# Output jobs of one unit moved behind the next unit's query jobs, x loaded transposed, two job banks

## The reference, cut to what matters

```
h    = rms_norm(x, norm_gain)
proj = h @ w_in                       # 5632 columns: aq ak av ag | rq rk rv rg
attn = window_attention(aq, ak, av)   # 16 heads of 64, 4 key/value heads, chunks of 64, window of 2 chunks,
                                      # q and k normed per head, bias -slope*|distance|, one sink per head
ret  = retention(rq, rk, rv)          # 8 heads, q/k 64 wide, v 128 wide, state carried from chunk to chunk,
                                      # group norm per head
out  = x + concat(attn * silu(ag), ret * silu(rg)) @ w_out
```

## Time and profile before

| | |
|---|---|
| Time, median of 3 runs | 1658.97 us (1658.12 to 1659.2) |
| The profiled execution, its own time | 1657.89 us |
| Its span, from the first to the last instruction | 1656.1 us |
| Mean granted clock of TensorE, share of full speed | 0.996 |
| PE busy | 1598.1 us (96%) |
| DVE busy | 1166.8 us (70%) |
| ACT busy | 673.7 us (41%) |
| POOL busy | 450.8 us (27%) |

### The profile page before, as it was taken

How to read it: one execution, slowest core, us unless ns; L and a number is a source line. 1 busy time by engine, 2 the same in 40 slices (tenths; PEclk the granted TensorE clock), 3 DMA queues, 4 the chain that set the end, 5 groups by cost and what they waited for, 6 DMA issues and landing times.

```text
span 1656.1 us, 24605 instructions
## 1 busy us (share of the span) xinstructions
PE 1598.1 (96%) x8320; PEld 1380.1 (83%) x8320; DVE 1166.8 (70%) x3045; ACT 673.7 (41%) x1985; POOL 450.8 (27%) x453
## 2 busy tenths in 40 slices
PE   5999999999999999999999999999999999999999
PEld 5778788787798888888888898888888888888887
DVE  6887768867868576684776757576686766757576
ACT  6543635535444242432444334241444414334241
POOL 5546446454412111121211212121121111212111
PEclk9999999999999999999999999999999999999999
DMA  9748567575774443546357353443547445353451
GB/s 309 280 147 309 200 215 267 185 249 206 245 293 145 176 180 125 200 156 216 125 196 286 135 203 139 170 191 118 213 171 267 181 173 189 129 203 133 171 197 51
DMA packets 151453, 320.49 MB, mean 194 GB/s; under 512 B 26272, under 2 KB 89888, under 8 KB 151328
## 3 DMA queue, kind: packets, MB, share of 16 engines
q1 hardware_dynamic: 151328, 318.91, 53.9%
HBM read 247.56 MB, written 71.30 MB: 193 GB/s over the span
## 4 chain that ended last, share of the span: by engine, by line
PE 51%; DVE 29%; ACT 13%; issue 5%; POOL 1%; DMA 0%; SPq 0%; DVEq 0%; ACTq 0%
PE jb L902 15%; PE jb L904 15%; PE jb L903 14%; ACT sx L417 6%; DVE sx L632 3%; DVE m L635 3%; DVE sx L630 2%; DVE qS L610 2%; DVE d L640 2%; DVE pTL L560 1%; DVE rawqn L603 1%; DVE rawqn L600 1%; ACT qS L400 1%; POOL rstd L303 1%; PE s L975 1%
## 5 line engine op out<-in xcount | busy, mean ns | idle before, releaser
L902 PE MATMUL jb<-wH,hTH 128*128 128x512 f32 (+1 forms) x1024 | 373.8, 365 | 0.0
L903 PE MATMUL jb<-wL,hTH 128*128 128x512 f32 (+1 forms) x1024 | 372.0, 363 | 0.0
L904 PE MATMUL jb<-wH,hTL 128*128 128x512 f32 (+1 forms) x1024 | 371.9, 363 | 0.0
L902 PE MATMUL jb<-wH,mxH 128*128 128x512 f32 x512 | 206.7, 404 | 10.8 <-DVE mxL L560 10.7
L904 PEld LDWEIGHTS jb<-wH,hTL 128*128 128x128 f32 x1024 | 192.8, 188 | 20.5
L902 PEld LDWEIGHTS jb<-wH,hTH 128*128 128x128 f32 x1024 | 193.4, 189 | 18.6
L903 PEld LDWEIGHTS jb<-wL,hTH 128*128 128x128 f32 x1024 | 193.0, 188 | 18.2
L902 PE MATMUL jb<-hTH,wH 128*128 128x512 f32 x512 | 203.4, 397 | 4.0 <-DVE gate L653 4.0
L903 PE MATMUL jb<-hTL,wH 128*128 128x512 f32 x512 | 201.2, 393 | 0.0
L904 PE MATMUL jb<-hTH,wL 128*128 128x512 f32 x512 | 201.1, 393 | 0.0
L904 PE MATMUL jb<-wH,mxL 128*128 128x512 f32 x512 | 200.6, 392 | 0.0
(11 more groups left out here) (148 smaller groups left out, 2973.6 us busy)
## 6 DMA issues: line engine op xcount, KB each, us to landing
wH<-scrH SPq DMA_DIRECT2D x144, 512.0 KB, 7.4
wL<-scrL SPq DMA_DIRECT2D x144, 512.0 KB, 8.1
scrH<-wH SPq DMA_DIRECT2D x48, 512.0 KB, 5.3
scrL<-wL SPq DMA_DIRECT2D x48, 512.0 KB, 6.0
wH<-scrH SPq DMA_DIRECT2D x48, 384.0 KB, 5.8
wL<-scrL SPq DMA_DIRECT2D x48, 384.0 KB, 6.5
stage<-w_in_dram SPq DMA_DIRECT2D x64, 256.0 KB, 4.5
acc<-x_dram SPq DMA_DIRECT2D x4, 2048.0 KB, 15.2
```

The costliest lines, as they stand in the source:

```text
L902: pe.matmul(o, lh, rh_, start=i == 0, stop=False)
L903: pe.matmul(o, lh, rl_, start=False, stop=False)
L904: m = pe.matmul(o, ll, rh_, start=False, stop=i == last)
```

## The change

- The order of the jobs. Unit 0 does query, gate, value jobs. Units 1 to 14 do their query jobs, then the 8 output jobs of the unit before, then their gate and value jobs. Unit 15 does query, gate and value jobs, then the output jobs of 14 and of 15. The jobs still alternate between two banks.
- The steps. The end of the retention of the unit before (A 3, I 2, I 3, MT 0 and 1) stands between the query jobs of this one, MT 2 and 3 and the score steps of this unit between the output jobs. DVE, ACT and POOL have new orders to fit, one part for the query jobs (`qkv_phase`), one for the output jobs, one for gate and value jobs (`late_phases`).
- x. A host-made transposed copy `xT` is loaded to `xt`. PE transposes only the broadcast scale of a tile (`XB`, 1 transpose for each tile instead of 8), DVE multiplies `xt` by gain and scale (`h`), ACT makes the H part in two instructions for a tile, POOL (in block 0 DVE) the L part in two.
- Weights are laid out by panel in HBM by the host, so that a chunk of a panel is one transfer instead of up to three; `stage` has 3 chunks instead of 4. The two weight buffers go by the order of the panels.
- `bias` is 256 columns wide; the mask of the first chunk of block 0 is a DVE memset in units 0 to 3. The small softmax tiles (`m4`, `nm4`, `d4`, `den`, `es`, `rc`) have a copy for even and odd t; `qS` has 2 instead of 4. The scores' two halves stay in separate columns of PSUM, as before.
- `tr` is freed by whichever of TQ and MT used it last (`tr_free`).

```diff
+def phases(n):
+    if n == 0:
+        return [("Q", 0), ("G", 0), ("V", 0)]
+    if n < LAST:
+        return [("Q", n), ("O", n - 1), ("G", n), ("V", n)]
+    return [("Q", n), ("G", n), ("V", n), ("O", n - 1), ("O", n)]
...
+STEPS_MID = {("Q", 0): [("A", -1, 3)], ("Q", 1): [("I", -1, 2), ("MT", -1, 0)], ("Q", 2): [("MT", -1, 1), ("I", -1, 3)],
+             ("Q", 3): [("TQ", 0, 0)],
+             ("O", 0): [("TQ", 0, 1)], ("O", 1): [("MT", -1, 2), ("S", 0, 0)], ("O", 2): [("MT", -1, 3)],
+             ("O", 3): [("TQ", 0, 2), ("S", 0, 1)], ("O", 5): [("TQ", 0, 3), ("PT", 0, 0)],
+             ("O", 6): [("S", 0, 2)], ("O", 7): [("PV", 0, 0)],
+             ("G", 0): [("PT", 0, 1), ("S", 0, 3)], ("G", 3): [("PV", 0, 1), ("PT", 0, 2)],
+             ("V", 0): [("PV", 0, 2)], ("V", 1): [("PT", 0, 3), ("A", 0, 0)],
+             ("V", 2): [("PV", 0, 3), ("A", 0, 1), ("I", 0, 0)], ("V", 3): [("A", 0, 2), ("I", 0, 1)]}
...
 POOL
+            def qkv_phase(n):                       # m = n - 1
+                wl(m, 3, (0, 1)); ggm(m, 3)
+                rpow(n, 0); gpow(m, 1); wl(m, 3, (2, 3))
+                rpow(n, 1); gpow(m, 2); wl(m, 3, (4, 5))
+                rpow(n, 2); wl(m, 3, (6, 7)); gpow(m, 3)
+                rpow(n, 3)
...
 ACT
+            def ocopy(n, t):                        # as before: waits for s_mr of t - 1
+            def qkv_phase(n):
+                rvg(m, 3); ocopy(m, 1); rh(m, 2); wh(m, 3, (0, 1))
+                qkv(n, 0); rh(m, 3); kwh_ah(m, 3); mth(m, 0); ocopy(m, 2); wh(m, 3, (2, 3))
+                qkv(n, 1); mth(m, 1); ocopy(m, 3); wh(m, 3, (4, 5))
+                qkv(n, 2); tqh(n, 0); wh(m, 3, (6, 7))
+                qkv(n, 3); tqh(n, 1); mth(m, 2)
...
+                exps(n, 0); wh(n, 1, (0, 1)); mth(n - 1, 3)
+                tqh(n, 2); exps(n, 1); wh(n, 1, (2, 3))
+                tqh(n, 3); pth(n, 0); exps(n, 2); wh(n, 1, (4, 5))
+                pth(n, 1); wh(n, 1, (6, 7))
...
 DVE
+            def h(b, t):
...
+                for k in range(KT):
+                    i = v.scalar_tensor_tensor(out=xt[:, t % 2, k], in0=xt[:, t % 2, k], scalar=ngain[:, k:k + 1],
+                                               in1=factor, op0=ALU.mult, op1=ALU.mult)
...
+            def qkv_phase(n):
+                rvg(m, 3); kw_am(m, 3); gna(m, 1); rl(m, 2)
+                if n % NU == 0:
+                    h(n // NU, 3)
+                qkv(n, 0); rupd(m, 2); rl(m, 3); kwl_al(m, 3); gnv(m, 1); mtl(m, 0); gnb(m, 1); gna(m, 2)
+                qkv(n, 1); gnv(m, 2); mtl(m, 1); rupd(m, 3); carry_in(n); gnb(m, 2); gna(m, 3)
+                qkv(n, 2); gnv(m, 3); tql(n, 0)
+                qkv(n, 3); tql(n, 1); mtl(m, 2); gnb(m, 3)
+            def late_phases(n):
+                add(n - 1, 7); ptl(n, 1); part1(n, 3); part2(n, 2); carry_out(n); agg(n, 0); rl(n, 0)
+                part2(n, 3); agg(n, 1)
+                mix(n, 0)
+                rq_decay(n)
+                mix(n, 1); ptl(n, 2)
+                mix(n, 2)
+                rvg(n, 0); ptl(n, 3); kw_am(n, 0); kwl_al(n, 0)
+                rvg(n, 1); mix(n, 3); rupd(n, 0); kw_am(n, 1); rl(n, 1); kwl_al(n, 1); gna(n, 0)
+                rvg(n, 2); gnv(n, 0); rupd(n, 1); kw_am(n, 2); kwl_al(n, 2); gnb(n, 0)
...
+            for n in range(1, LAST):
+                qkv_phase(n)
+                part1(n, 0); add(m, 0); mtl(m, 3); add(m, 1)
+                tql(n, 2); part1(n, 1); add(m, 2); part2(n, 0); add(m, 3)
+                tql(n, 3); add(m, 4); ptl(n, 0); part1(n, 2); add(m, 5); part2(n, 1); add(m, 6)
+                late_phases(n)
...
 PE
             def bank_free(n, j):
+                i = JOB_AT[n, j]                    # waits for the reader of the job two before in the new order
...
+            def tr_free():
+                if tr_user[0]:
+                    pe.wait_ge(S[tr_user[0][0]], tr_user[0][1])
...
-            def XT(b, t):
-                for k in range(KT):
-                    m = pe.transpose(xbanks[t % 2][k // 4][:, (k % 4) * P:(k % 4 + 1) * P],
-                                     xbuf[t % 2][:, k * P:(k + 1) * P], ident[:, :])
+            def XB(b, t):
+                pe.transpose(bank, xr[:, t:t + 1].broadcast_to([P, P]), ident[:, :]).then_inc(S["s_xb"], 1)
```

More of the change, by code:

```diff
@@ L252, in units @@
[L252 to L269 removed]
+                    sp.wait_ge(S["s_acc"], b * 32 + 24 + 2 * (t + 1))
@@ new lines, in _ @@
+            xpow(0, 0)
+            wl(0, 0, range(4))
+            xpow(0, 1)
+            wl(0, 0, range(4, 8))
+            xpow(0, 2)
+            xpow(0, 3)
+            qkv_phase(0)
+            late_phases(0)
+            for n in range(1, LAST):
+                qkv_phase(n)
+                if n % NU == 2 and n // NU < NB - 1:
+                    for t in range(NT):
+                        xpow(n // NU + 1, t)
+                wl(n, 1, range(8))
+                late_phases(n)
+            n, m = LAST, LAST - 1
@@ new lines, in _ @@
+            v.wait_ge(S["s_gains"], 16)
+            xms_(0, 0)
+            h(0, 0)
+            xms_(0, 1)
+            xl_first(0)
+            h(0, 1)
+            xl_first(1)
+            xms_(0, 2)
+            xms_(0, 3)
+            h(0, 2)
+            xl_first(2)
+            v.wait_ge(S["s_qkg"], 64)
+            carry_in(0)
+            qkv(0, 0)
+            h(0, 3)
+            xl_first(3)
+            qkv(0, 1)
+            qkv(0, 2); tql(0, 0)
+            qkv(0, 3); tql(0, 1); part1(0, 0)
@@ new lines, in _ @@
+            agg(0, 0); tql(0, 2); part2(0, 0); part1(0, 1)
+            agg(0, 1); tql(0, 3); part2(0, 1); rq_decay(0); ptl(0, 0); part1(0, 2)
+            mix(0, 0); ptl(0, 1); part2(0, 2); part1(0, 3); carry_out(0)
+            mix(0, 1); rl(0, 0); ptl(0, 2); kw_am(0, 0); kwl_al(0, 0); rvg(0, 0); part2(0, 3)
+            mix(0, 2); ptl(0, 3); kw_am(0, 1); rvg(0, 1); rupd(0, 0); rl(0, 1); kwl_al(0, 1); gna(0, 0)
+            mix(0, 3); rvg(0, 2); gnv(0, 0); rupd(0, 1); kw_am(0, 2); kwl_al(0, 2); gnb(0, 0)
@@ new lines, in _ @@
+            n, m = LAST, LAST - 1
+            qkv_phase(n)
+            part1(n, 0); agg(n, 0); mtl(m, 3); tql(n, 2); part2(n, 0); part1(n, 1)
+            agg(n, 1); tql(n, 3); part2(n, 1); part1(n, 2)
+            rq_decay(n); ptl(n, 0); part2(n, 2); part1(n, 3)
+            rl(n, 0); mix(n, 0); part2(n, 3)
+            kw_am(n, 0); kwl_al(n, 0); rvg(n, 0); ptl(n, 1)
+            kw_am(n, 1); rvg(n, 1); rupd(n, 0); rl(n, 1); kwl_al(n, 1); gna(n, 0)
+            kw_am(n, 2); rvg(n, 2); rupd(n, 1); rl(n, 2); kwl_al(n, 2); gnv(n, 0); gnb(n, 0); gna(n, 1)
@@ L831, in _ @@
+            rvg(n, 3); kw_am(n, 3); gnv(n, 1)
+            add(m, 0); rupd(n, 2); rl(n, 3); kwl_al(n, 3); gnb(n, 1); gna(n, 2); add(m, 1)
+            mtl(n, 0); mix(n, 1); ptl(n, 2); gnv(n, 2); add(m, 2); rupd(n, 3); gnb(n, 2); gna(n, 3); gnv(n, 3)
+            add(m, 3); mix(n, 2); mtl(n, 1); ptl(n, 3); gnb(n, 3); add(m, 4); add(m, 5); mtl(n, 2)
+            mix(n, 3); add(m, 6); add(m, 7); mtl(n, 3)
+            for i in range(8):
+                add(n, i)
         @block.tensor
         def _(pe):
-            pe.sem_inc(S["s_job"], CREDIT_JOB)
@@ L924, in S_ @@
                     for hp in range(2):
-                        m = pe.matmul(s_parts[:, par, hp], qS[:, t, 2 * hp + par], kHL[:, :, win], start=True, stop=True)
+                        m = pe.matmul(s_parts[:, par, hp], qS[:, t % 2, 2 * hp + par], kHL[:, :, win], start=True, stop=True)
                 m.then_inc(S["s_s"], 1)
```

820 lines of the change are left out of this document (453 added, 367 removed), and 12 rows, old and new, of tables (STEPS_FIRST, STEPS_LAST).

## The result

The changed kernel takes 1909.03 us (median of 4 runs, 1906.95 to 1912.98), the kernel before 1658.88 beside it: a ratio of 1.1512 (1.1492 to 1.1531). It is 250 us slower, where 136 were forecast: the direction was right, the size was not, and the time lies outside the range given (1705 to 1865 us).

The account below looks back on a forecast made before the run. PE's work was taken as the bound, DVE next behind it. From the profiled span, 1656 - 12 - 9 + 35 - 3 + 110 + 3 + 4 + 10 = 1794, with about 2 around the span: 1795 us, range 1705 to 1865.

Parts of the forecast that it names:

- The gates of a later unit: Units 4 to 14, query and output jobs: PE stalls until DVE is done, 11.7 us a unit, net +10.
- TQ 1: PE step among the query jobs: waits for `tql(n,0)` to empty the shared bank `tr`; stall 2.8 us.
- +35: Units 1 to 3: same stalls plus weight splitting, 22.5 us against 8.9 + 1.9 before; +12 each, range 0 to +55.
- +113: Units 4 to 14: net +10 for each of 11 units (+110), and +3 for block turns in units 4, 8, 12.
- the term of the clock: Whole kernel: work lost at the lowered clock after stalls, up to 1.7 us a fall; +10 in all (0 to +95).
- the last unit (+4): Unit 15: two query-job gates, late `part1` and `tql`, then 16 output jobs with late DVE adds; +4 (0 to +12).
- unit 4 (+1 above the others): Block turn: `h(b,3)` before the first query tile, `xh` before the second; +1 beyond a middle unit's net +10.
- -12 and -9: Savings: -12 at the start (-5 to -16) from shorter tile preparation, -9 at later blocks from fewer transposes of x.
- at nothing: Bias, mask, small-tile edits, new waits of `mixh` and `mth`, SP reloads and fewer weight transfers: counted as no time.
- Rival 3: Each stall of 2 us or more costs the full 1.7 by the clock, four a unit: +95, 1880 us; chance 0.1.
- The splitting's term: Units 1 to 3: ACT and POOL queues 2.8 us up to `tql(n,0)`, DVE's slowdown 8 us in query and output jobs.
- Tile 3: Start, unit 0: x tile ready near 27 us, its `h` behind DVE's first query tile; fourth job ends near 31.

Follow-up runs that it names:

- experiment 2: Changed kernel with PE running unread identity transposes ahead of its five long waits in units 1 to 14; 1878.67 us, ratio 1.1322.
- Experiment 1: Changed kernel with the old order of jobs, steps and engine lists, all other edits kept; 1662.62 us, ratio 1.0028 to the kernel before.
- Experiment 8: Old order with the other edits, plus S ahead of TQ, next block's first `h` behind `gna(3)`, XB(2) and XB(3) later; 1665.94 us, ratio 1.0048.

## Why the prediction was wrong

**What held.** The bound and the direction: PE had nothing to win and DVE's order sets it back. The gates of a later unit: named in place and order, at most 10.3 us (a unit of experiment 2 against one of before) against 11.7, from the terms of the earlier trace rows; I 3's was not seen. TQ 1 looks off by more than half (1.2 us for 2.8), but only because PE comes late to it at the low clock: at the full clock of experiment 2 it would have waited from 753.33 to 755.34, 2.0 us. The rows of before were enough to do this by hand. The waits held beyond the later units, too: from before to after PE's idle time grew by 39.3 us in units 1 to 3 (20.1 to 59.4), where +35 was forecast, and by 105 us in units 4 to 14 (9.2 to 114.3), where +113 was.

**What failed.** First of all the term of the clock: PE's busy time, for which the forecast had +10 by the clock and -9 by the turns, grew by 80 us. Then the last unit (+4), unit 4 (+1 above the others) and what the other edits were to bring (-12 and -9).

**The other edits, missed by 25 us.** They were to bring -12 at the start and -9 at the turns, and nothing else. Experiment 1 has all of them and is 4.5 us slower than before: the turns gave back 4.3 in all, the start 2.6, and against these stand 0.5 us in each later unit and 4.3 in unit 0, which "at nothing" left out.

**The clock, mis-sized.** "+10 in all (0 to +95)" was taken on the ground that much of a fall would lie ahead of a gate that DVE sets anyway. That reason is the step that failed, and the two falls of a later unit show how. The second one comes behind o4, with no gate after it: half of its 3.4 us, 1.7, is lost in full (an estimate). The first lies ahead of TQ 1, as was reckoned, but DVE does not set that gate alone: it needs the third query tile, and the query job that the low clock slows delivers it. DVE's wait for it in the changed kernel, and the same instruction in experiment 2:

```profile
758.89 0.49 DVE L767 TENSOR_REDUCE ss<-th 128x5 f32<-128x320 f32 x1 [2.20 <-ACT th L519]
750.93 0.49 DVE L767 TENSOR_REDUCE ss<-th 128x5 f32<-128x320 f32 x1
```

From the start of MT 1 to DVE's last instruction ahead of TQ 1 it takes 15.3 us here and 13.2 there. So 2.2 us of the fall go through, and some 0.8 are hidden in TQ 1's shorter wait. Together 3.9 us a unit, where experiment 2 measured at least 3.5. In the whole kernel experiment 2 gives 30 us, with 126 of 236 low microseconds taken away; at that ratio, 0.24 a microsecond, all of it is some 57 us (an estimate). Rival 3 (+95, "each stall of 2 us or more") was too high, the forecast far too low. A later unit has two such falls and not four: TQ 1's 1.2 us and o2's 1.5 were followed by none.

**Units 1 to 3: the waits right, the clock missing.** +35 was forecast, +58.5 came: 39.3 of it is PE's idle time, and 19.2 its busy time, with 65 us at the low clock instead of 10. No run separates the clock's share in these units as experiment 2 does in the later ones. The splitting's term (2.8 + 8 a unit) is not refuted: with a quarter of the splitting the three units are 34 us above before instead of 58.5, so three quarters of it cost some 8 us a unit, its part in the clock's falls included. Beside the gates of a later unit PE waits in unit 2 for `pTL` in PV, longer for `tql` at TQ 1, and in the first gate jobs eight times for POOL's low halves:

```profile
PE ob L1187 <- DVE pTL L736: 4.5, 1, 4.5
PE tr L1151 <- DVE kHL L795: 3.7, 1, 3.7
PE jb L1134 <- POOL wL L381: 3.6, 8, 1.2
```

**Unit 4, mis-sized.** +23.9 came, where 10 had been put down and 1 for the turn. `xl(2)`, `xl(3)` and the last `wl` are ahead of POOL's powers and `h(3)` is ahead of the query tiles, and the first two gates alone are 14.4:

```profile
PE tr L1234 <- DVE mr L930: 7.5, 1, 7.5
PE tr L1151 <- DVE kHL L795: 6.9, 1, 6.9
```

The first of them is `h(3)`. DVE's eight instructions took 6.8 us here, beside POOL's `xl` and `wl`, and ACT's read of the first query job waited 6.3 us for them. In experiment 1 eight such instructions took 2.2 us where POOL had no work beside them:

```profile
503.50 6.81 DVE L965 SCALAR_TENSOR_TENSOR xt<-xt,ngain,rawqn 128x128 f32<-128x128 f32 x8
```

In units 8 and 12, which turn a block but split nothing, `h(3)` took 3.7 us, and MT 1 waited 4.4 instead of 2.2. With a quarter of the splitting `h(3)` of unit 4 took 5.2 us and the unit lost 4.3. Of the second gate, 6.9 us for 1.2, no run shows the parts.

**The last unit, mis-sized.** +4 (0 to +12) was set without following its lists as the middle unit's were. They have a gate in nearly every phase:

```profile
PE tr L1151 <- DVE mxL L736: 5.0, 1, 5.0
PE tr L1234 <- DVE kHL L795: 3.6, 1, 3.6
PE ab L1201 <- DVE amr L883: 3.5, 1, 3.5
...
1776.00:1850.00 74.00, 56.94 (x244) 46.89 (x244) 33.41 (x87) 21.51 (x72) 6.65 (x6) 0.84 0.31 114
```

(The last line is a stretch: clock 0.84.) Of the +44.2 us of the two end units, 21.6 are waits of this one, and it has 30.7 us at the low clock, up to 15 us of work lost (an estimate, half of them). No run changed its lists, so the cause is read from the waits alone.

**The start, wrong in a step.** Tile 3 was to be ready near 27 and the fourth job to end near 31; it ended at 41. The step that failed is the start of the first job. Tile 0 was reckoned ready near 10, but all four transposes XB stand ahead of the first job, and the last of them needs POOL's power of tile 3:

```profile
22.36 0.47 PE L1245 MATMUL s<-ident,xr 128*128 128x128 f32 x1 [0.79 <-POOL xr L420]
```

From 22.5 on PE does the four jobs without a wait, 18.5 us, in the first 2.7 of them with a start every 0.32 us: that alone gives 41. Experiment 8 shows that a second limit lies just behind: with two XB moved the first job begins 8 us earlier and the fourth ends no earlier, since it waits 4.1 us for ACT's read of the second, and ACT had waited 6.5 us for `h(0,3)`. That is behind the first query tile on DVE, and the tile behind `carry_in(0)`, which waits for a small constant:

```profile
27.67 0.17 DVE L752 TENSOR_SCALAR nsink<-sink 128x2 f32<-128x2 f32 x1 [2.47 <-DMA sink<-sink_logits_dram]
```

The forecast had named the query tile ahead of `h(0,3)`, but not the load ahead of both. In the changed kernel PE waits for neither.

**In one sentence:** the gates of the steady part were reckoned and came out within 2 us a unit; the parts that were estimated instead of followed (the clock, unit 4, the two ends) were all too small, above all the clock, whose falls slow the very jobs that DVE's next gate waits for.

## What to carry to other kernels

When PE is full and another engine has two thirds of its work, ask of a new order which stretch gets that engine's work, and follow both lists gate by gate; waits of 1 to 3 us then come out well from the trace of before. Put the clock into the sum as its own term wherever such waits stand close together, and follow through the list what a slowed job hands on late. Reckon first, last and loading units by the same method as the middle one, since they cost some 100 of 255 us here. If the order must stay, take the long pieces (here scores) from between the short ones that free a bank: that alone gave back 88 of 250 us, and an early group norm another 26.

## Not expected of the hardware

Single waits of 2.2 us (with one of 0.7 behind it) and of 2.6 us each came with a fall of the granted clock, for 6.8 and 3.4 us, in most later units; filling them with transposes that nothing reads made the kernel 30 us faster. Two DVE operations with both inputs in SBUF took a third longer beside POOL's splitting, while one with an input in PSUM kept its time to 1 ns; and `h(3)`, 2.2 us for eight instructions without POOL's work beside them, took 6.8 with it in unit 4.
